# Two layers of a hybrid attention and feed-forward block: the output projection in quarter projections, the normed input of the feed-forward kept in SBUF, and the last additions on GpSimd

## The reference, cut to what matters

```python
mix = y @ w_out                                              # token_mix, 1024 x 1024
x = x + gate_mix * rms_norm(mix, g_post_mix)
h = rms_norm(x, g_pre_ffn) * (1 + scale_ffn) + shift_ffn     # modulate
z = dwconv(h @ w_up, w_conv, b_conv)                         # 1024 x 5632, three taps along the tokens
g, val = split(z, 2)
f = (silu(g) * val) @ w_down                                 # 2816 x 1024
x = x + gate_ffn * rms_norm(f, g_post_ffn)
```

## Time and profile before

| what | value |
|---|---|
| median of three runs | 4011.78 us (4011.36 to 4012.75) |
| the profiled execution | 4007.81 us |
| its span, first to last instruction | 4006.0 us |
| mean granted clock of TensorE | 0.927 |
| PE busy | 3350.1 us, 84% of the span |
| DVE, ACT, POOL busy | 2018.1, 1232.3 and 716.9 us |
| DMA | 342.64 MB, 86 GB/s over the span |

### The profile page before, as it was taken

The page is one execution under the profiler, slowest core; times in us unless marked ns, Lnnn a source line. Parts: engine busy times, 40 slices in busy tenths (PEclk is TensorE's granted clock), DMA queues, the critical chain, the costliest instruction groups (busy, mean ns, idle before and its releaser), DMA issues. The chain is left out here.

```text
span 4006.0 us, 46136 instructions
## 1 busy us (share of the span) xinstructions
PE 3350.1 (84%) x16882; PEld 2586.9 (65%) x16882; DVE 2018.1 (50%) x2714; ACT 1232.3 (31%) x1830; POOL 716.9 (18%) x884
## 2 busy tenths in 40 slices
PE   5398968778684999999998498787876679999997
PEld 0187845555473888888886386655555567777775
DVE  1266546666342444544445465656663434444445
ACT  0143245555231221111212242455552221212121
POOL 0033434444101000000001132444441100000001
PEclk7598979999897999999999698999998889999999
DMA  9544210000346111111112444100003441111112
GB/s 382 201 165 165 86 51 28 27 29 7 115 156 191 42 39 45 37 31 37 37 42 80 163 169 152 64 18 29 26 7 115 174 130 42 52 42 52 42 47 105
DMA packets 200655, 342.64 MB, mean 86 GB/s; under 512 B 23864, under 2 KB 145920, under 8 KB 184672
## 3 DMA queue, kind: packets, MB, share of 16 engines
q1 hardware_dynamic: 200544, 341.20, 24.6%
HBM read 254.03 MB, written 87.13 MB: 85 GB/s over the span
## 5 line engine op out<-in xcount | busy, mean ns | idle before, releaser
L1911 DVE TENSOR_TENSOR ff_acc<-ff_dn,ff_acc 128x512 f32<-128x512 f32 x396 | 271.9, 690 | 328.1 <-PE ff_dn L123 327.8
L121 PE MATMUL ff_z_gate<-ff_hT,ff_u_hi 128*128 128x512 f32 (+1 forms) x880 | 331.6, 377 | 76.2 <-DMA ff_hT<-hT_d 76.2
L121 PE MATMUL ff_dn<-ff_d_lo,ff_a_hi 128*128 128x512 f32 x792 | 320.1, 404 | 32.7 <-issue 17.0
L123 PE MATMUL ff_z_gate<-ff_hT,ff_u_hi 128*128 128x512 f32 (+1 forms) x880 | 329.7, 375 | 0.0
L1796 POOL TENSOR_TENSOR ff_ms<-ff_ss,c_eps 128x1 f32<-128x1 f32 x18 | 19.8, 1101 | 1730.2 <-ACT ff_t_gate L1874 1730.2
L122 PE MATMUL ff_z_gate<-ff_hT,ff_u_lo 128*128 128x512 f32 (+1 forms) x880 | 328.8, 374 | 0.0
L121 PE MATMUL ff_z_value<-ff_hT,ff_u_hi 128*128 128x512 f32 (+1 forms) x880 | 327.1, 372 | 0.0
L123 PE MATMUL ff_z_value<-ff_hT,ff_u_hi 128*128 128x512 f32 (+1 forms) x880 | 326.6, 371 | 0.0
L122 PE MATMUL ff_z_value<-ff_hT,ff_u_lo 128*128 128x512 f32 (+1 forms) x880 | 325.7, 370 | 0.0
L1897 DVE SCALAR_TENSOR_TENSOR ff_t_gate<-ff_z_gate,c_vec,ff_t_gate 128x1023 f32<-128x1023 f32 (+1 forms) x132 | 132.1, 1015 | 362.9 <-ACT ff_t_gate L1849 356.1
L122 PE MATMUL ff_dn<-ff_d_hi,ff_a_lo 128*128 128x512 f32 x792 | 310.5, 392 | 0.0
(11 more groups left out here) (256 smaller groups left out, 7320.3 us busy)
## 6 DMA issues: line engine op xcount, KB each, us to landing
mod_wm<-in_w_mod_dram SPq DMA_DIRECT2D x48, 1024.0 KB, 7.9
ff_u_raw<-in_w_up_dram SPq DMA_DIRECT2D x88, 512.0 KB, 3.8
ff_d_raw<-in_w_down_dram SPq DMA_DIRECT2D x44, 512.0 KB, 4.4
...
```

Source lines behind the costliest of these rows:

```text
L121: e.matmul(out, w[0], x[1], start=start, stop=False)
L123: return e.matmul(out, w[0], x[0], start=False, stop=stop)
L1911: e.tensor_tensor(out, dn[:, half, :], out, ALU.add).then_inc(acc_done, 1)
```

## The change

The output projection is written anew, without the loop and the helper classes. The work of a slot i on TensorE is cut into four quarters of 12 matmuls, and the turns stand between them: quarter 0, half of y's turn of tile i + 1, quarter 1, half of xn's turn of tile i - 2, quarter 2, the other half of y's turn, quarter 3, the other half of xn's. w_out is loaded in four DMAs of 1 MB into a buffer of its full size, in which the low part takes the place of the raw one (`pair`). y is loaded two tiles ahead; the sum with x is written into the buffer of x. h is written, split, into `hT` in SBUF, which now lies in an outer phase around both; `hT_d` is no longer stored here, nor loaded by the feed-forward. At the end of the feed-forward the addition of x moves from VectorE to GpSimd (`add_x`), behind the root of the tile two later. Removed lines of `mix_out_phase` are left out below, since the function before stands above.

```diff
     def sb(self, name, shape, dt=F32):
         return self.ctx.enter_context(self.nc.sbuf_tensor(f"{self.name}_{name}", shape, dt))
+    def next_place(self):
+        return -(-self.nc.sbuf_base // 32) * 32
+    def pair(self, raw, rounded, shape):
+        base = self.next_place()
+        tile = self.sb(rounded, shape, F32R)
+        return self.nc.alloc_sbuf_tensor_at(f"{self.name}_{raw}", shape, F32, offset=base), tile
     def ps(self, name, shape, dt=F32):
         return self.ctx.enter_context(self.nc.psum_tensor(f"{self.name}_{name}", shape, dt))
...
-def mix_out_phase(nc, l, c, t0, inp, mod_d, y_d, x_of, xs_d, hT_d):
...
+def mix_out_phase(nc, l, c, t0, inp, mod_d, y_d, x_of, xs_d, hT):
+    N, LAG = NT - t0, 2
     with Phase(nc, f"mo{l}") as ph:
...
+        w_raw, w_lo = ph.pair("w_raw", "w_lo", [P, KD, D])
+        w_hi = ph.sb("w_hi", [P, KD, D], F32R)
+        hf = ph.sb("hf", [P, KD, P])
...
+        gates_sync, gates_vector = gates(ph, inp, mod_d, l, GATE_MIX, "g_post_mix", G, hf[:, :, :].rearrange("p k f -> p (k f)"))
+        y, x, xn = ph.sb("y", [P, 2, D]), ph.sb("x", [P, 2, D]), ph.sb("xn", [P, 2, D])
         ys = ph.sb("ys", [P, 2, 2, KD, P], F32R)
...
+        yT, op, hp = ph.ps("yT", [P, KD, P]), ph.ps("op", [P, 2, D]), ph.ps("hT_turn", [P, KD, P])
...
+        def stream(i):
+            return CTXV if i + t0 < CT else LATV
         @block.sync
         def _(e):
...
+            def load_y(i):
+                if i >= 2:
+                    e.wait_ge(y_turned, 2 * (i - 2) + 2)
+                e.dma_start(y[:, i % 2, :], y_d[i + t0]).then_inc(y_in[i % 2], 16)
+            def load_x(i):
+                if i >= 2:
+                    e.wait_ge(x_stored[i % 2], 16 * (i // 2))
+                    e.wait_ge(xn_done, i - 1)
+                e.dma_start(x[:, i % 2, :], x_of(i + t0)).then_inc(x_in[i % 2], 16)
+            def store(i):
+                e.wait_ge(sum_done, i + 1)
+                e.dma_start(xs_d[i + t0], x[:, i % 2, :]).then_inc(x_stored[i % 2], 16)
+            load_y(0)
+            for i in range(KD // 2):
+                e.dma_start(w_raw[:, 2 * i:2 * i + 2, :], w_v[:, 2 * i:2 * i + 2, :]).then_inc(w_in[i], 16)
+            load_y(1)
+            load_x(0)
+            gates_sync(e)
+            load_x(1)
+            for i in range(N + 1):
+                if 2 <= i + 2 < N:
+                    load_y(i + 2)
+                if i >= 1:
+                    store(i - 1)
+                if 2 <= i + 1 < N:
+                    load_x(i + 1)
             for u in range(2):
...
+                e.wait_ge(x_stored[u], 16 * (N // 2))
         @block.scalar
         def _(e):
...
+            def y_hi(i, h):
+                e.wait_ge(y_turned, 2 * i + h + 1)
+                if i >= 2 and h == 0:
+                    e.wait_ge(mm_done, i - 1)
+                e.copy(ys[:, i % 2, 0, 4 * h:4 * h + 4, :], yT[:, 4 * h:4 * h + 4, :]).then_inc(ys_hi, 1)
+            def split_w(k):
+                e.wait_ge(w_in[k // 2], 16)
+                e.copy(w_hi[:, k, :], w_raw[:, k, :]).then_inc(w_hi_done, 1)
+            def square_o(i):
+                u = i % 2
+                e.wait_ge(mm_done, i + 1)
+                if i >= 2:
+                    e.wait_ge(h_turned, 2 * (i - 2) + 2)
+                e.activation(xn[:, u, :], op[:, u, :], ACT.Square, scale=D ** -0.5, accum_out=sso[:, u:u + 1]).then_inc(sqo_done, 1)
+            def square_x(i):
+                u = i % 2
+                e.wait_ge(sum_done, i + 1)
+                e.activation(xn[:, u, :], x[:, u, :], ACT.Square, scale=D ** -0.5, accum_out=ssx[:, u:u + 1]).then_inc(sqx_done, 1)
+            def norm(i):
+                u = i % 2
+                e.wait_ge(sqx_done, i + 1)
+                e.wait_ge(stx_done, 2 * i + 2)
+                e.mul(xn[:, u, :], x[:, u, :], rsx[:, u:u + 1]).then_inc(xn_done, 1)
+            def hi(i, h):
+                e.wait_ge(mod_done, KD * i + 4 * h + 4)
+                e.copy(hT[:, 0, 4 * h:4 * h + 4, i * P:(i + 1) * P], hf[:, 4 * h:4 * h + 4, :]).then_inc(hi_done, 1)
+            split_w(0)
+            for h in range(2):
+                y_hi(0, h)
+            for k in range(1, KD):
+                split_w(k)
+            for i in range(N + LAG):
+                if 0 <= i - 1 < N:
+                    square_o(i - 1)
+                if i + 1 < N:
+                    y_hi(i + 1, 0)
+                if 0 <= i - 1 < N:
+                    square_x(i - 1)
+                if 0 <= i - LAG < N:
+                    hi(i - LAG, 0)
+                if 0 <= i - 1 < N:
+                    norm(i - 1)
+                if i + 1 < N:
+                    y_hi(i + 1, 1)
+                if 0 <= i - LAG < N:
+                    hi(i - LAG, 1)
         @block.gpsimd
         def _(e):
...
+            def stats(i, sums, means, roots, squared, done):
+                u = i % 2
+                e.wait_ge(squared, i + 1)
+                e.tensor_tensor(means[:, u:u + 1], sums[:, u:u + 1], c.eps[:, 0:1], ALU.add).then_inc(done, 1)
+                e.wait_ge(done, 2 * i + 1)
+                e.tensor_tensor(roots[:, u:u + 1], means[:, u:u + 1], c.minus_half[:, 0:1], ALU.pow).then_inc(done, 1)
+            for i in range(N):
...
         @block.tensor
         def _(e):
...
+            def turn_y(i, h):
+                if h == 0:
+                    e.wait_ge(y_in[i % 2], 16 * (i // 2) + 16)
+                if i:
+                    e.wait_ge(ys_lo, 2 * (i - 1) + h + 1)
+                for k in range(4 * h, 4 * h + 4):
+                    ins = e.transpose(yT[:, k, :], y[:, i % 2, k * P:(k + 1) * P], c.ident[:, :])
+                ins.then_inc(y_turned, 1)
+            def turn_h(i, h):
+                if h == 0:
+                    e.wait_ge(xn_done, i + 1)
+                if i:
+                    e.wait_ge(mod_done, KD * (i - 1) + 4 * h + 4)
+                for k in range(4 * h, 4 * h + 4):
+                    ins = e.transpose(hp[:, k, :], xn[:, i % 2, k * P:(k + 1) * P], c.ident[:, :])
+                ins.then_inc(h_turned, 1)
+            def project(i, q):
+                u, a = i % 2, 512 * (q // 2)
+                if q == 0 and i >= 2:
+                    e.wait_ge(tn_done, i - 1)
+                if q < 2:
+                    e.wait_ge(ys_lo, 2 * i + q + 1)
+                for k in range(4 * (q % 2), 4 * (q % 2) + 4):
+                    if i == 0 and q < 2:
+                        e.wait_ge(w_lo_done, k + 1)
+                    ins = product(e, op[:, u, a:a + 512], (ys[:, u, 0, k, :], ys[:, u, 1, k, :]),
+                                  (w_hi[:, k, a:a + 512], w_lo[:, k, a:a + 512]), k == 0, k == KD - 1)
+                if q == 3:
+                    ins.then_inc(mm_done, 1)
+            for h in range(2):
+                turn_y(0, h)
+            for i in range(N + LAG):
+                for q in range(4):
+                    if i < N:
+                        project(i, q)
+                    if q % 2 == 0 and i + 1 < N:
+                        turn_y(i + 1, q // 2)
+                    if q % 2 == 1 and 0 <= i - LAG < N:
+                        turn_h(i - LAG, q // 2)
         @block.vector
         def _(e):
...
+            def y_lo(i, h):
+                ks = slice(4 * h, 4 * h + 4)
+                e.wait_ge(ys_hi, 2 * i + h + 1)
+                e.tensor_tensor(ys[:, i % 2, 1, ks, :], yT[:, ks, :], ys[:, i % 2, 0, ks, :], ALU.subtract).then_inc(ys_lo, 1)
+            def split_w(k):
+                e.wait_ge(w_hi_done, k + 1)
+                e.tensor_tensor(w_lo[:, k, :], w_raw[:, k, :], w_hi[:, k, :], ALU.subtract).then_inc(w_lo_done, 1)
+            def residual(i):
+                u = i % 2
+                e.wait_ge(sto_done, 2 * i + 2)
+                e.scalar_tensor_tensor(out=xn[:, u, :], in0=op[:, u, :], scalar=rso[:, u:u + 1], in1=G[:, stream(i), :],
+                                       op0=ALU.mult, op1=ALU.mult).then_inc(tn_done, 1)
+                e.wait_ge(tn_done, i + 1)
+                e.wait_ge(x_in[u], 16 * (i // 2) + 16)
+                e.tensor_tensor(x[:, u, :], xn[:, u, :], x[:, u, :], ALU.add).then_inc(sum_done, 1)
+            def modulate(i, h):
+                v = stream(i)
+                e.wait_ge(h_turned, 2 * i + h + 1)
+                if i:
+                    e.wait_ge(lo_done, 2 * (i - 1) + h + 1)
+                for k in range(4 * h, 4 * h + 4):
+                    e.tensor_scalar(hf[:, k, :], hp[:, k, :], c.ab[:, v, 1, 0, k:k + 1], c.ab[:, v, 1, 1, k:k + 1],
+                                    ALU.mult, ALU.add).then_inc(mod_done, 1)
+            def lo(i, h):
+                ks, at = slice(4 * h, 4 * h + 4), slice(i * P, (i + 1) * P)
+                e.wait_ge(hi_done, 2 * i + h + 1)
+                e.tensor_tensor(hT[:, 1, ks, at], hf[:, ks, :], hT[:, 0, ks, at], ALU.subtract).then_inc(lo_done, 1)
+            split_w(0)
+            for h in range(2):
+                y_lo(0, h)
```

(58 more changed lines are left out.)

115 lines of the change are left out of this document (11 added, 104 removed).

## The result

The kernel after takes 3910.11 us (median of four runs, 3908.19 to 3911.46), the one before 4012.27 on the same chip; the ratio is 0.9744, with a 95% interval of 0.9728 to 0.9761. Forecast were 3924.4 us and a range of 3900 to 3950. The profiled execution has a span of 3907.8 us, 98.2 less than before; forecast were 87.4. TensorE is busy for 3329.1 us, 85% of it, and the DMAs move 304.90 MB instead of 342.64.

A forecast was written before the change was run, and what follows sets the result against it. TensorE is busy for 84% of the span, so what counts is where it is not. Gains of 54.6 us (first layer) and 48.3 (second), less 15.5, give 87.4: from 4011.8 to 3924.4 us, range 3900 to 3950.

The forecast's parts named there:

- Slots: Output projection's slots: a full slot takes 13.1 us with y no longer late; 16.1 us gained in first layer, 10.0 in second.
- rival C: Output projection: the chain of small steps, not TensorE, sets a slot; 3945 us, chance 0.10.
- the 1.3 us: Full slot of the output projection: time left free, as the chain of small steps takes 11.8 of 13.1 us.
- Head: Start of the output projection: w_out loads without waits let slot 1 start earlier; 5.2 us gained in each layer.
- the 2.2 us added for a slow clock: Head of the output projection: allowance because TensorE has hardly warmed up in the last two quarters.
- Tail: End of the output projection: without h's last store, 18.7 us instead of 26.8; 8.1 gained in each layer.
- Start of the feed-forward: Up to z_gate complete: the wait for hT goes; 25.2 us gained in first layer, 25.0 in second.
- Last sums: Feed-forward's end: VectorE's scaling and GpSimd's addition exclude each other, about 4.3 us a tile against 3.66; 15.5 us lost.
- Rival B: Last sums: shared access costs nothing and the loads of x bind; about 4 us lost, 3913 us, chance 0.10.
- rival B2: Last sums: VectorE's sums from PSUM are held up too, 5.7 us a tile; 3946 us, chance 0.06.
- D: z_gate and the first slot: TensorE stays at 1.2 GHz throughout; 3949 us, chance 0.07.
- E: Output projection's slots: waits on SyncE's queue make the kernel slower than before, 4034 us at 20 us a slot; chance 0.03.

The follow-up runs named there:

- x later: Kernel before, with y's load first in a slot and x's load one slot later; 3980.02 us, ratio 0.9919.
- whole turns: Kernel after, with the turns of y and xn uncut at the start of a slot, from slot 1 on; 3901.2 us, ratio 0.9723.
- the ring: Kernel after, with the third and fourth w_out loads held until earlier low parts are done, as the four buffers did; 3920.84 us, ratio 0.977.
- h by way of DRAM: Kernel after, with h stored to DRAM by the output projection and loaded again by the feed-forward; 3963.93 us, ratio 0.9876.
- taking the part back: Kernel after, with the addition of x at the end of the feed-forward on VectorE again; 3897.27 us, ratio 0.9716.
- making it alone: Kernel before, with only the addition of x at the end of the feed-forward moved to GpSimd; 4026.75 us, ratio 1.0034.
- gate in PSUM: Kernel after, with the product of gate and weight written to PSUM, so VectorE's scaling has one SBUF input; 3902.28 us, ratio 0.9731.

## Why the prediction was right

The sign, the range and every large term held. The median came 14.3 us below the forecast: 10.8 by the ledger, and 3.5 because the profiled execution of before lay 4.0 below its median, that of after (3907.8 + 1.8) only 0.5. Of the 10.8, 2.1 are the earlier start of the output projection, which is drift and no merit of the change.

**Slots.** Right in mechanism: no wait for y, xn or `ys`, and a granted clock of 1.00. x later in the old kernel shows the cause by itself, 27.1 us where the forecast had 26.1. The size was 12.83 us and not 13.1, under the bound of 12.9 that I gave; with the two shorter slots this makes 2.8 + 2.4 us more. Part of the error is the price of xn's turn: it holds the next turn off by 0.88 us (1099.67 to 1100.55 with x later), not 1.03. The rest lies in the projection itself, since with whole turns the old code takes 12.98 us for a slot and the new one 12.64: its 48 matmuls, in the same order, follow one another every 0.234 us in the old code and every 0.227 in the new. What shortens that step I did not isolate; the stores of h are not it, as the slot is 12.83 with them back. The chain of small steps, rival C, does not bind; how much of the 1.3 us was left free I have not measured.

**Head.** Right cause (the ring costs 10.7 us when it is put back), low by 3.7 us in the first layer. The low parts ended 17.8 us after SyncE's first load (1059.46) instead of 18.8, and the second quarter lay closer behind them; above all the 2.2 us added for a slow clock did not come in the second half, since the matmuls were at 0.40 us from 1054.87 on, 3.9 us after the first. In the second layer y of tile 1 was 2.17 us late, and the matmuls behind that wait were at 0.63 us again, which took some of this back.

**Tail.** 18.7 us forecast, 18.67 and 18.68 measured, and not by chance: the last low part ends 17.75 us after the last turn of a full slot (1197.01), 17.5 in the forecast, and the barrier takes 0.92 instead of 1.2. What the forecast did not see is that part of it is made by the change itself: xn's last turn stands at the end of a slot, and one place earlier the tail is shorter.

**Start of the feed-forward.** The first layer as forecast: the first matmul 6.4 us after the phase's start (6.1 forecast), z_gate 15.7 long (16.3). h by way of DRAM confirms the term, 53.8 us against 50.2 and the 7.6 for the last store of h in the tails. In the second layer the first matmul came 8.3 us after the start, 2.2 later than forecast, behind the load of w_up; why that load took longer there I did not test.

**Last sums.** 15.5 us forecast, 15.3 measured, 12.8 by taking the part back and 14.5 by making it alone. The mechanism is right, and that the total is so close is in part luck. The steps in a tile one after another were to give 4.3 us and gave 4.12, which is 2.2 us less over twelve tiles. The scaling adds only 1.08 us behind GpSimd's addition, and GpSimd's mean ends with the scaling and not 0.19 behind it; the addition itself took 2.41 us (2.35 forecast, 2.25 by the estimate beside it). The ends cost 2.0 us more than forecast; in them the last addition waits 1.38 and 2.03 us for its load of x. Rival B (shared access free) is refuted by the 3.00 us, rival B2 by VectorE's sums from PSUM, 0.69 us inside an addition. The Trainium skill ("SBUF — State Buffer", Who interferes with whom) says that an instruction of VectorE with a single SBUF input takes no part in the exclusion; the prediction had no long overlap for this half, and the traces now agree: 1.27 us for the scaling with its gate in PSUM inside an addition of 2.41.

**Rivals D and E.** TensorE did not stay at 1.2 GHz. Its matmuls went from 0.63 to some 0.40 us 3.9 us after the first of the head (1050.97 to 1054.87), and 4.0 and 4.4 us after the first of z_gate (1204.35 to 1208.34 in the first layer); in the slots the granted clock is 1.00. SyncE's waits delayed no engine in the slots.
